# The last gate row's sums inside the attention, and plain heads that come out of the values product already turned

## The chip, the cores and the metric

The kernel is one program on 1 core of a Trainium2 chip. The metric is the device time of one launch in microseconds (us). The kernel before was timed three times: median 944.96 us, lowest 944.74, highest 946.05.

## What is computed

The reference is two layers of a diffusion backbone over 256 latent and 256 context tokens of width 1024, everything in float32. Layer 0 is a convolution and pooling mixer followed by a mixture of experts. Layer 1 is attention followed by a mixture of experts, and it gives out the latent tokens only. Every sublayer has a norm, a shift and scale from conditioning vectors (six rows per layer: shift, scale and gate of either sublayer), and a gate on its output. What matters here is cut from the reference:

```
def attend(q, k, v, scale):
    s = einsum(q, k) * scale
    p = softmax(s)
    return einsum(p, v)

o_m = attend(q_m, k_m, v_m, MLA_SCALE)                  # 4 plain heads
a1, a2 = attend(q1, k1, v_d, ..), attend(q2, k2, v_d, ..)
o_d = rms_norm(a1 - lam * a2, g_sub) * (1.0 - lam_init) # 4 differential heads
y = concatenate([o_m, o_d]) @ w_out
x = x + mod[1, 2] * y
x = x + mod[1, 5] * moe(modulate(rms_norm(x), mod[1, 3], mod[1, 4]))
```

The moe of a layer has 32 experts in 8 groups of 4; a token uses 2 experts of one group. All the weights of every expert are read once in a layer, whatever tokens it gets.

## The kernel before, in words

Each engine runs one program that is written out by hand, and semaphores order them. The names below are the kernel's.

**Weights.** SyncE (SP) issues all weight transfers in the order of `stream_plan` (133 units of up to 2 MB, numbered n below). `slot_plan` gives every unit a place: seven ring slots (0 to 6) and, for expert weights alone, four lent places: WORK_SLOT (7), X_SLOT (8), B_SLOT (9), PART_SLOT (10). SP goes through the units in order and, ahead of each, waits until the place is free (`load`, with `freed` for what the last unit of that place was read by); so a unit that has to wait holds all later ones. Units 81 and 82 are the two halves of `mod 1 5`, the weights of the moe gate row of layer 1. Units 83 and 84 are `wout`, the output projection of layer 1. From unit 85 on come the experts of layer 1: 85 `gu 0`, 86 `gu 1`, 87 `gu 2`, 88 `gu 3`, 89 `down 0`, 90 `gu 4`, 91 `gu 5`, 92 `down 1`, 93 `gu 6`, 94 `gu 7`, 95 `down 2`. With these eleven units all eleven places are full; unit 96 needs the place of unit 85, which is free when the first expert step is done. Before, 88 goes to WORK_SLOT and 89 to B_SLOT, and both wait for the last `o_turned` of the attention; 90 and 91 go to slots 6 and 3, which held units 81 and 82 and are free when these have been summed.

**Conditioning rows of layer 1.** Rows 2 to 5 are products of a vector of 1024 with a 1024 x 1024 matrix, made on VectorE: `mod_sum(n)` (L1882) multiplies a 128x512 piece of the weights with a per-partition scalar and adds it to a running sum (L1897; the first of a row is the plain product, L1895). Each row takes 16 such passes. The 48 passes of rows 2, 3 and 4 lie between the steps of the layer's projections. The 16 passes of row 5 (n = 48 to 63) stand in `add_out(1)`, ahead of the first two output tiles: ten ahead of tile 0 and six ahead of tile 1. TensorE adds up the partitions in `sum_moe_rows` (L1067, the product L1072) after the third tile of the output projection (`project_out`, L1150).

**Attention.** There are 16 units in `UNITS`: 0 to 7 plain (a head and a block of 128 queries each), 8 to 15 differential (two maps each). The engines run a software pipeline over an index i:

- TensorE (`attention_pe`), in iteration i: `probs(i-2)` turns the map, four 128x128 transposes (L570); `scores(i+1)`, for the plain units two at a time (L552, L555), for the differential ones four 64-row products (L561); `values(i-3)` (L581), whose stationary operand is the turned map and whose moving operand is the values, so that the result has queries in rows; `turn_o(i-5)` (L588) turns this result back.
- VectorE (`attention_vector`), in iteration i: `output_rows(i-3)` multiplies the result by one over the sum of the map's row (L1844; L1842 in the differential heads, with the norm's factor, too); `maxima(i+2)` (L1816, L1818); `normalize(i+1)` (L1825 takes the reciprocal of the sum; for a differential unit L1828 and L1830 form the difference of the two maps). The maps of the plain units are not divided before they are turned.
- ScalarE (`attention_scalar`), in iteration i: `exps(i)` (L664), `o_squares(i-3)` in the differential heads (L680), `o_cols(i-5)` copies the turned result to `oT` (L672), `turned_probs(i-1)` (L686).
- GpSimd takes the root for the differential heads and, before the attention, fetches the bias of row 5 into WORK (L2378).

`link` makes the next VectorE instruction wait for the one before it.

**After the attention** come the output projection in four tiles (L1150), the second norm, the router, then rows stored to memory and gathered by expert group, and the 16 expert steps, in each of which TensorE needs two `gu` units and one `down` unit.

## Time and profile before

| | |
|---|---|
| median of three runs | 944.96 us (944.74 to 946.05) |
| the profiled execution's own time | 942.52 us |
| its span | 940.9 us |
| mean granted TensorE clock | 0.956 of full speed |
| busy: TensorE, VectorE, ScalarE, GpSimd | 840.2, 362.6, 168.2, 178.1 us |
| moved by DMA | 297.99 MB, 317 GB/s on average |
| attention (first score product to last turned result) | 615.2 to 669.3 us of the span |
| output projection (L1150) | 669.4 to 700.0 us of the span |

The profile is of one execution. Its span leaves out 1.6 us that the execution's own time has. Times in the rows below are from the start of the span. A row of a timeline has the start, the duration, the engine, the line and the shapes; instructions of one group that follow each other are merged, with their number, and then the duration is that of the whole run. PE is TensorE, PEld its weight loads, DVE VectorE, ACT ScalarE, POOL GpSimd, SPq the queue of SyncE.

### The profile page before, as it was taken

The numbers are of one execution on the slowest core, as the hardware profiler recorded it, in microseconds if no ns is written. First come the engines' busy times: TensorE is split into PE (matmuls) and PEld (weight loads), VectorE is DVE, ScalarE is ACT, GpSimd is POOL, SyncE is SP. The second block draws the span as 40 slices with busy tenths as digits, with TensorE's granted clock in tenths as the row PEclk, the third lists the DMA queues.
The fourth block names the chain that finished last, engine by engine and source line by source line (L and its number), as shares of the span: only waits on it lengthen the run. The fifth ranks groups of instructions, "written<-read, shape, count | busy, mean of one in ns | idle before, by whom it ended". The sixth has DMA issues, their size and how long they took to land.

```text
span 940.9 us, 10044 instructions
## 1 busy us (share of the span) xinstructions
PE 840.2 (89%) x3735; PEld 372.3 (40%) x3735; DVE 362.6 (39%) x764; ACT 168.2 (18%) x415; POOL 178.1 (19%) x214
## 2 busy tenths in 40 slices
PE   4899999999999999878859999789899999778886
PEld 1444445447433333223238444446445333222222
DVE  1279998217111211110223686648624111111011
ACT  2301012216100000000032111538323000000000
POOL 2100292221220222211131321401211111011001
PEclk9999999999999999999959999989999999889888
DMA  8999354717999999999989469310577999999993
GB/s 363 409 416 399 142 213 194 286 72 277 339 402 400 365 405 395 401 397 418 420 329 424 163 231 370 134 71 1 212 302 257 408 400 406 416 418 424 414 417 162
DMA packets 34038, 297.99 MB, mean 317 GB/s; under 512 B 6624, under 2 KB 6930, under 8 KB 16316
## 3 DMA queue, kind: packets, MB, share of 16 engines
q1 hardware_dynamic: 26928, 283.26, 74.8%
q0 software_dynamic: 6976, 13.93, 4.2%
q8 instruction: 38, 0.62, 0.3%
q14 instruction: 20, 0.16, 0.0%
q10 hardware_dynamic: 76, 0.02, 0.0%
HBM read 293.67 MB, written 12.58 MB: 325 GB/s over the span
## 4 chain that ended last, share of the span: by engine, by line
PE 47%; DMA 24%; DVE 12%; issue 5%; SPq 5%; ACT 3%; PEld 2%; POOL 1%; PEldq 0%; DVEq 0%; POOLq 0%; ACTq 0%
PE bank L1275 11%; DVE WORK L2210 10%; DMA ring<-in_gu_pack 9%; PE bank L495 9%; PE bank L1300 6%; PE bank L1425 5%; DMA B<-in_gu_pack 5%; SPq L975 5%; DMA ring<-in_down_pack 4%; DMA ring<-in_win_pack 3%; PE bank L1150 3%; PE bank L1372 2%; PE bank L581 2%; DMA h_rows<-B 1%; PE bank L552 1%
## 5 line engine op out<-in xcount | busy, mean ns | idle before, releaser
L1275 PE MATMUL bank<-ring,hT 128*64 128x512 f32 x704 | 220.0, 633 | 25.1 <-DMA ring<-in_gu_pack 12.8
L2124 DVE SCALAR_TENSOR_TENSOR hT<-hT,WORK,bank 128x256 f32<-128x256 f32 x34 | 16.3, 481 | 326.3 <-ACT hT L1575 326.3
L1275 PEld LDWEIGHTS bank<-ring,hT 128*64 128x64 f32 x704 | 64.5, 145 | 125.2 <-issue 124.7
L2210 DVE SCALAR_TENSOR_TENSOR WORK<-WORK,par 128x512 f32<-128x512 f32 x116 | 90.7, 858 | 0.0
L495 PE MATMUL bank<-ring,hT 128*128 128x512 f32 (+2 forms) x256 | 88.0, 499 | 0.7 <-ACT hT L1538 0.7
L1300 PE MATMUL bank<-ring,WORK 128*64 128x512 f32 x336 | 76.3, 596 | 2.8 <-DMA ring<-in_down_pack 1.7
L1275 PE MATMUL bank<-WORK,hT 128*64 128x512 f32 x128 | 63.9, 645 | 5.0 <-issue 3.5
L1580 ACT ACTIVATE WORK<-bank 128x256 f32<-128x256 f32 x34 | 13.1, 384 | 282.9 <-PE bank L1284 282.9
L495 PEld LDWEIGHTS bank<-ring,hT 128*128 128x128 f32 x256 | 46.0, 190 | 35.8 <-issue 34.0
L1372 PE MATMUL bank<-hT,ring 128*128 128x512 f32 x128 | 57.7, 610 | 1.9 <-DMA ring<-in_win_pack 1.9
L1425 PE MATMUL bank<-ring,B 128*128 128x512 f32 x128 | 56.6, 596 | 0.8 <-DVE B L2227 0.8
L1275 PE MATMUL bank<-X,hT 128*64 128x512 f32 x104 | 49.5, 622 | 5.9 <-issue 3.1
L857 POOL DMA_INDIRECT hT<-h_rows,smalli x21 | 20.1, 959 | 174.2 <-PE bank L1249 80.5
L2255 POOL TENSOR_SCALAR small<-small 128x1 f32<-128x1 f32 (+2 forms) x46 | 13.5, 294 | 181.4 <-DVE small L1739 62.5
L1275 PE MATMUL bank<-B,hT 128*64 128x512 f32 x96 | 43.6, 597 | 1.0 <-issue 1.0
L1034 PE MATMUL bank<-ring,cs 128*32 128x512 f32 x256 | 33.9, 666 | 9.7 <-DMA ring<-in_mod_pack 8.5
L1300 PEld LDWEIGHTS bank<-ring,WORK 128*64 128x64 f32 x336 | 23.2, 137 | 45.1 <-issue 40.9
L1372 PEld LDWEIGHTS bank<-hT,ring 128*128 128x128 f32 x128 | 24.6, 195 | 33.4 <-issue 30.9
L870 POOL DMA_INDIRECT latents<-WORK,smalli x8 | 8.2, 1023 | 153.5 <-DVE WORK L2142 153.5
L2256 POOL TENSOR_TENSOR small<-small,cst 128x1 f32<-128x1 f32 (+2 forms) x46 | 35.8, 777 | 3.8
L1425 PEld LDWEIGHTS bank<-ring,B 128*128 128x128 f32 x128 | 23.8, 190 | 31.2 <-issue 27.7
L1575 ACT ACTIVATE hT<-bank 128x256 f32<-128x256 f32 x34 | 13.1, 384 | 124.9 <-PE bank L1275 121.0
(312 smaller groups left out, 1086.0 us busy)
## 6 DMA issues: line engine op xcount, KB each, us to landing
ring<-in_gu_pack SPq DMA_DIRECT2D x39, 2048.0 KB, 21.3
ring<-in_mod_pack SPq DMA_DIRECT2D x24, 2048.0 KB, 11.5
ring<-in_down_pack SPq DMA_DIRECT2D x19, 2048.0 KB, 25.5
WORK<-in_gu_pack SPq DMA_DIRECT2D x6, 2048.0 KB, 23.5
ring<-in_wout_pack SPq DMA_DIRECT2D x4, 2048.0 KB, 12.7
ring<-in_gu_pack SPq DMA_DIRECT2D x8, 1024.0 KB, 28.6
ring<-in_win_pack SPq DMA_DIRECT2D x3, 2048.0 KB, 37.0
X<-in_gu_pack SPq DMA_DIRECT2D x3, 2048.0 KB, 29.8
```

What stands on the lines that cost most here:

```text
L495: mm = pe.matmul(dst[:, 0:hi - lo], hT[:, k, t * P:(t + 1) * P], w[:, k, :], start=k == 0, stop=k == KC - 1)
L581: mm = pe.matmul(bank[VBANK[i % 2]][:, 0:P], PT[i % 2][:, c * P:(c + 1) * P], v[:, c, h * P:(h + 1) * P], start=c == 0, stop=c == 3)
L857: return pool.indirect_dma_start(XG[s], None, h2d[:, :], bass.IndirectOffsetOnAxis(ap=smalli[0:ST, i:i + 1], axis=0), bounds_check=rows_ - ...
L975: sp.dma_start(dst, src).then_inc(sem(f"weights_in{at}"), 16)
L1034: mm = pe.matmul(bank[b][at:at + 32, :], cs[:, k, :], w, start=k < 2, stop=k >= KC - 2)
L1150: mm = pe.matmul(bank[OUT_BANKS[L][i % 2]][:, :], lhs(k, j), w[:, k, :], start=k == 0, stop=k == KC - 1)
L1275: mm = pe.matmul(dst[ST * x:ST * x + ST, :], HG[L][s][:, k, :], columns(units[x], 512 * k, 512), start=k == 0, stop=k == KC - 1)
L1300: mm = pe.matmul(bank[5 + s][ST * h:ST * h + ST, :], HET[s][:, f, ST * x:ST * x + ST], columns(n, 2048 * x + 1024 * f + 512 * h, 512), sta ...
L1372: mm = pe.matmul(b[:, :], w[:, k, 256 * part + P * (m % 2):256 * part + P * (m % 2) + P], hT[:, k, :], start=k == 0, stop=k == KC - 1)
L1425: mm = pe.matmul(bank[OUT_BANKS[0][i % 3]][:, :], mixT[:, (k + 4) % KC, j * P:(j + 1) * P], w[:, (k + 4) % KC, :], start=k == 0, stop=k == ...
L2210: ins = dve.scalar_tensor_tensor(out=acc, in0=src, scalar=w, in1=acc, op0=ALU.mult, op1=ALU.add)
L2256: pool.tensor_tensor(dst, dst, C("half", 0, 1).to_broadcast([P, n]), ALU.pow).then_inc(sem(name), 1)
```

## The change

Three things are edited.

1. The 16 `mod_sum` passes of row 5 leave `add_out(1)` and stand in VectorE's attention loop, two behind `normalize(i+1)` in each of the iterations 0 to 7.
2. In the plain units the map is divided by its sum ahead of the turn: behind the reciprocal comes a `link` and a 128x512 multiplication in place on VectorE. `values` then takes the values as stationary operand and the turned map as moving operand, so that the result has queries in columns. `output_rows` and `turn_o` are left out for units 0 to 7, and ScalarE copies the result from its bank to `oT` at i-3 instead of i-5.
3. In `slot_plan` the places of `mod 1 5` no longer count as late. Units 88 and 89 then go to slots 6 and 3, and 90 and 91 to WORK_SLOT and B_SLOT; the same four places trade their later units in the same way. The wait of the lent places is for 8 `o_turned` instead of 16, since only the differential units are turned.

The diff:

```diff
--- before.py
+++ after.py
@@ -181,7 +181,7 @@
         if n > where_second and (not expert or WORK_SLOT not in free):
             free.sort(key=order)
         if expert and WORK_SLOT not in free:
-            late = [at for at in free if stream[held[at]][0] == "wout" or stream[held[at]][:3] == ("mod", 1, 5)]
+            late = [at for at in free if stream[held[at]][0] == "wout"]
             soon = [at for at in free if at not in late]
             if u[1] == 0:
                 free = soon + [WORK_SLOT] + late + [X_SLOT, B_SLOT, PART_SLOT]
@@ -351,6 +351,7 @@
         MOD_BANK = (6, 6, 6, 6, 6, 6, 7, 6)
         PBANK = (0, 1, 4, 5)
         VBANK = (5, 7)
+        PLAIN = 8
 
         UNITS = [(0, 2 * a + b, t) for a in range(2) for t in range(2) for b in range(2)] + [(1, h, t) for h in range(4) for t in range(2)]
 
@@ -573,17 +574,22 @@
             def values(i):
                 d, h, t = UNITS[i]
                 pe.wait_ge(sem("pt_done"), i + 1)
-                if i >= 2:
-
-                    pe.wait_ge(sem("o_rows"), i - 1)
-                v = VD if d else VM
+                if 2 <= i < PLAIN + 2:
+
+                    pe.wait_ge(sem("o_cols"), i - 1)
+                elif i >= 2:
+                    pe.wait_ge(sem("o_rows"), i - 1 - PLAIN)
                 for c in range(4):
-                    mm = pe.matmul(bank[VBANK[i % 2]][:, 0:P], PT[i % 2][:, c * P:(c + 1) * P], v[:, c, h * P:(h + 1) * P], start=c == 0, stop=c == 3)
+                    p, v = PT[i % 2][:, c * P:(c + 1) * P], (VD if d else VM)[:, c, h * P:(h + 1) * P]
+                    if d:
+                        mm = pe.matmul(bank[VBANK[i % 2]][:, 0:P], p, v, start=c == 0, stop=c == 3)
+                    else:
+                        mm = pe.matmul(bank[VBANK[i % 2]][:, 0:P], v, p, start=c == 0, stop=c == 3)
                 mm.then_inc(sem("pv_mm"), 1)
 
             def turn_o(i):
-                pe.wait_ge(sem("o_rows"), i + 1)
-                if i:
+                pe.wait_ge(sem("o_rows"), i + 1 - PLAIN)
+                if i > PLAIN:
                     pe.wait_ge(sem("o_cols"), i)
                 pe.transpose(bank[6][:, 0:P], OR[i % 2], ident).then_inc(sem("o_turned"), 1)
 
@@ -597,7 +603,7 @@
                     values(i - 3)
                 if i == n_units + 2:
                     sum_rows()
-                if 0 <= i - 5:
+                if PLAIN <= i - 5:
                     turn_o(i - 5)
 
         def attention_scalar(act, gate_rows):
@@ -667,15 +673,19 @@
 
             def o_cols(i):
                 d, h, t = UNITS[i]
-                act.wait_ge(sem("o_turned"), i + 1)
-                scale = subs[:, 0:1] if d else 1.0
-                act.activation(oT[:, 4 * d + h, t * P:(t + 1) * P], bank[6][:, 0:P], ACT.Identity, scale=scale).then_inc(sem("o_cols"), 1)
+                to = oT[:, 4 * d + h, t * P:(t + 1) * P]
+                if d:
+                    act.wait_ge(sem("o_turned"), i + 1 - PLAIN)
+                    act.activation(to, bank[6][:, 0:P], ACT.Identity, scale=subs[:, 0:1]).then_inc(sem("o_cols"), 1)
+                else:
+                    act.wait_ge(sem("pv_mm"), i + 1)
+                    act.activation(to, bank[VBANK[i % 2]][:, 0:P], ACT.Copy).then_inc(sem("o_cols"), 1)
 
             def o_squares(i):
                 j = i % 2
                 act.wait_ge(sem("pv_mm"), i + 1)
-                if i >= 2:
-                    act.wait_ge(sem("o_turned"), i - 1)
+                if i >= PLAIN + 2:
+                    act.wait_ge(sem("o_turned"), i - 1 - PLAIN)
                 u = 2 * (i % 8)
                 act.activation(OR[j], bank[VBANK[j]][:, 0:P], ACT.Square, scale=ri[:, u:u + 1], accum_out=oss[:, j:j + 1]).then_inc(sem("o_squares"), 1)
 
@@ -688,9 +698,11 @@
             for i in range(n_units + 5):
                 if i < n_units:
                     exps(i)
-                if 0 <= i - 3 < n_units and UNITS[i - 3][0]:
+                if PLAIN <= i - 3 < n_units:
                     o_squares(i - 3)
-                if 0 <= i - 5:
+                elif 0 <= i - 3 < PLAIN:
+                    o_cols(i - 3)
+                if PLAIN <= i - 5:
                     o_cols(i - 5)
                 if 0 <= i - 1 < n_units:
                     turned_probs(i - 1)
@@ -945,7 +957,7 @@
                 elif at == WORK_SLOT and STREAM[n][1] == 0:
                     sp.wait_ge(sem("mix_done"), 4)
                 elif at == WORK_SLOT or at == B_SLOT and STREAM[n][1] == 1:
-                    sp.wait_ge(sem("o_turned"), len(UNITS))
+                    sp.wait_ge(sem("o_turned"), len(UNITS) - PLAIN)
                 elif at == X_SLOT:
 
                     L = STREAM[n][1]
@@ -1829,28 +1841,30 @@
                                                   in1=es[:, o:o + 1], op0=ALU.mult, op1=ALU.mult))
                     ins = dve.scalar_tensor_tensor(out=EX[:, i % 2, 0, :], in0=EX[:, i % 2, 1, :], scalar=ri[:, u + 1:u + 2],
                                                    in1=EX[:, i % 2, 0, :], op0=ALU.mult, op1=ALU.add)
+                else:
+                    link(ins)
+                    ins = ts(EX[:, i % 2, 0, :], EX[:, i % 2, 0, :], ri[:, u:u + 1], None, ALU.mult)
                 ins.then_inc(sem("probs_ready"), 1)
 
             def output_rows(i):
                 dve.wait_ge(sem("pv_mm"), i + 1)
                 dve.wait_ge(sem("probs_ready"), i + 1)
                 scale = ri[:, 2 * (i % 8):2 * (i % 8) + 1]
-                if i >= 2:
-                    dve.wait_ge(sem("o_turned"), i - 1)
-                if UNITS[i][0]:
-                    dve.wait_ge(sem("o_rstd"), i - 7)
-                    ins = ts(OR[i % 2], bank[VBANK[i % 2]][:, 0:P], scale, ors[:, i % 2:i % 2 + 1], ALU.mult, ALU.mult)
-                else:
-                    ins = ts(OR[i % 2], bank[VBANK[i % 2]][:, 0:P], scale, None, ALU.mult)
-                ins.then_inc(sem("o_rows"), 1)
+                if i >= PLAIN + 2:
+                    dve.wait_ge(sem("o_turned"), i - 1 - PLAIN)
+                dve.wait_ge(sem("o_rstd"), i + 1 - PLAIN)
+                ts(OR[i % 2], bank[VBANK[i % 2]][:, 0:P], scale, ors[:, i % 2:i % 2 + 1], ALU.mult, ALU.mult).then_inc(sem("o_rows"), 1)
 
             for i in range(-2, n_units + 3):
-                if 0 <= i - 3:
+                if PLAIN <= i - 3:
                     output_rows(i - 3)
                 if i + 2 < n_units:
                     maxima(i + 2)
                 if 0 <= i + 1 < n_units:
                     normalize(i + 1)
+                if 0 <= i < KC:
+                    mod_sum(6 * KC + 2 * i)
+                    mod_sum(6 * KC + 2 * i + 1)
 
         @block.vector
         def _(dve):
@@ -1976,9 +1990,6 @@
                         last = i == 2 * nj - 1
                         if i >= 2:
                             dve.wait_ge(sem("x_added"), 8 * L + i - 1 + last)
-                        if L == 1 and i < 2:
-                            for n in (range(6 * KC, 6 * KC + 10), range(6 * KC + 10, 8 * KC))[i]:
-                                mod_sum(n)
                         dve.wait_ge(sem("out_mm"), 8 * L + i + 1)
                         tt(OUTT[L][i % 2], bank[OUT_BANKS[L][i % len(OUT_BANKS[L])]][:, :], GB[:, streams[j // 2], 512 * h:512 * h + 512], ALU.mult).then_inc(sem("out_used"), 1)
                         if last:
```

## Rows read from the trace of the kernel before

**Rows 1.** The page: the span

```profile
span 940.9 us, 10044 instructions
```

**Rows 2.** Chain that ended last, in time: start, us, what

```profile
649.94 1.06 PE bank L561 x4
651.00 1.09 PE bank L581 x8
652.20 0.44 PE bank L570 x4
...
669.38 22.56 PE bank L1150 x48
...
792.94 48.55 DMA ring<-in_gu_pack
```

**Rows 3.** Windows: busy of PE, PEld, DVE, ACT, POOL; clock, DMA share, GB/s

```profile
608.00:611.00 3.00, 1.37 (x6) 0.50 (x4) 2.52 (x10) 1.37 (x5) 1.28 (x3) 1.00 0.42 98
...
622.94:643.05 20.11, 19.33 (x113) 12.31 (x114) 11.20 (x34) 11.69 (x30) 0.00 (x0) 1.00 0.00 1
643.05:657.11 14.06, 14.06 (x92) 9.43 (x92) 13.53 (x36) 12.24 (x39) 2.25 (x6) 1.00 0.00 0
...
670.00:673.00 3.00, 3.00 (x5) 1.24 (x4) 2.67 (x5) 0.30 (x1) 0.00 (x0) 0.50 0.91 322
...
695.00:700.00 5.00, 5.00 (x14) 2.19 (x13) 0.00 (x0) 1.75 (x4) 0.74 (x2) 1.00 0.26 108
```

**Rows 4.** Timeline: VectorE's multiplications of 128x512, in the projections and in `add_out(1)`

```profile
566.98 0.88 DVE L1895 TENSOR_SCALAR B<-ring,cs 128x512 f32<-128x512 f32 x2
...
670.34 6.71 DVE L1897 SCALAR_TENSOR_TENSOR WORK<-ring,cs,WORK 128x512 f32<-128x512 f32 x10 [1.14 <-ACT GB L1557]
678.25 0.69 DVE L1983 TENSOR_TENSOR hT<-bank,GB 128x512 f32<-128x512 f32 x1 [1.20 <-PE bank L1150]
678.85 5.07 DVE L1897 SCALAR_TENSOR_TENSOR WORK<-ring,cs,WORK 128x512 f32<-128x512 f32 x6
```

**Rows 5.** Timeline of VectorE, a plain iteration (622.94) and an output row (628.82)

```profile
622.94 0.69 DVE L1816 TENSOR_REDUCE small<-bank 128x1 f32<-128x512 f32 x1 [1.08 <-PE bank L555]
623.74 0.15 DVE L1825 RECIPROCAL small<-small 128x1 f32<-128x1 f32 x1
623.81 0.67 DVE L1816 TENSOR_REDUCE small<-bank 128x1 f32<-128x512 f32 x1
...
628.82 0.35 DVE L1844 TENSOR_SCALAR WORK<-bank,small 128x128 f32<-128x128 f32 x1
629.09 0.68 DVE L1816 TENSOR_REDUCE small<-bank 128x1 f32<-128x512 f32 x1
```

**Rows 6.** Timeline of VectorE, one differential iteration, and the pass of L1842

```profile
643.05 1.27 DVE L1816 TENSOR_REDUCE small<-bank 128x1 f32<-128x512 f32 x2
644.44 0.16 DVE L1825 RECIPROCAL small<-small 128x2 f32<-128x2 f32 x1
644.63 0.22 DVE L1828 SCALAR_TENSOR_TENSOR small<-small 128x1 f32<-128x1 f32 x1
645.55 0.35 DVE L1844 TENSOR_SCALAR WORK<-bank,small 128x128 f32<-128x128 f32 x1
...
651.13 0.41 DVE L1842 TENSOR_SCALAR WORK<-bank,small 128x128 f32<-128x128 f32 x1
651.46 1.28 DVE L1816 TENSOR_REDUCE small<-bank 128x1 f32<-128x512 f32 x2
```

**Rows 7.** Timeline of SP's queue: start, time in the queue, units

```profile
668.95 0.33 SPq L975 DMA_DIRECT2D WORK<-in_gu_pack  x1
...
700.05 0.33 SPq L975 DMA_DIRECT2D ring<-in_gu_pack  x1
...
724.13 0.33 SPq L975 DMA_DIRECT2D B<-in_down_pack  x1
```

**Rows 8.** DMA issues, 560 to 800 us: size and median us to landing

```profile
WORK<-in_mod_b POOLq DMA_DIRECT2D x1, 4.0 KB, 2.1
```

## The prediction, made before the changed kernel was run

> **What bounds the kernel now.** I read the page first, for the span [rows 1], then the chain of waits in order of time, to see which stage is bound by what [rows 2]. Three stages matter. In the attention the chain stays on TensorE from product to product. In the output projection it is TensorE again: 48 products in 22.56 us. From 793 us it is a wait of 48.55 us for weights: the last fifth is bound by transfers. The windows [rows 3] then tell how full each engine is. From 622.94 to 643.05 TensorE is busy 19.33 of 20.11 us, and VectorE 11.20. From 643.05 to 657.11, the differential units, VectorE has 13.53 of 14.06: TensorE is full, and VectorE has hardly anything left either. That is what decides here, since the change puts work on VectorE at just this place.
>
> **Why the old place of the 16 passes costs nothing.** In the output projection ten passes take 6.71 us, and then VectorE waits 1.20 us for the first tile; six more follow in 5.07 us [rows 4]. TensorE needs about 7 us for a tile (22.56 us for three, with a slow start) and doesn't wait for them. Taking them out of there gains 0.
>
> **VectorE's new loop, iteration by iteration.** I take distances between starts, since durations overlap. A plain iteration of before: from the maximum (622.94) to the reciprocal (623.74) 0.80 us, then 0.07 to the next maximum (623.81) [rows 5]. New in it:
> - *The division.* It waits for the reciprocal. From a reciprocal to an instruction that waits for it are 0.19 us (644.44 to 644.63) [rows 6] instead of 0.07. The trace has no such division in place, but it has two products of 128x512 with a per-partition scalar, from SBUF to SBUF: 0.88 us for two, each 0.48 long, thus 0.40 from start to start [rows 4]. I take 0.40. Bounds: 0.27, the pitch of a 128x128 pass (628.82 to 629.09) [rows 5], and 0.66, that of the passes with two tensors (below).
> - *Two passes.* Ten take 6.71 us, the last of them 0.75 (their own duration; it moves the pitch by 0.01): 0.66 or 0.67 a pass, 1.33 for two. The six behind them have (5.07 - 0.75) / 5 = 0.86 a pass, while GpSimd adds tiles next to them [rows 4]. GpSimd is idle (0.00) in the new place from 622.94 to 643.05 [rows 3], so 0.66 holds there; 0.86 is the upper bound.
>
> So a plain iteration becomes 0.80 + 0.19 + 0.40 + 1.33 = 2.72 us, and there are six of them (iterations 0 to 5). Iteration 6 has the two maxima of a differential unit, 1.39 us to the reciprocal [rows 6], and divides the last plain map: 1.39 + 0.19 + 0.40 + 1.33 = 3.31. Iteration 7 is wholly differential; before, it takes 2.50 (643.05 to 645.55) without an output row [rows 6], with two passes 3.83. Sum: 6 x 2.72 + 3.31 + 3.83 = 23.46 us. Before, the same eight iterations take 643.05 - 622.94 = 20.11. VectorE comes to the maximum of unit 10 **3.35 us late**: 12.93 us of work are added (10.64 of passes, seven divisions at 0.52, less five output rows at 0.27), and of the 20.11 only 9.58 were idle (six times 0.87, 1.46, 2.50 and the five output rows are the rest).
>
> Do other engines hide or lengthen this? TensorE loses eight turns at 0.11 us (652.20 - 651.00 - 1.09 [rows 2]), 0.9 us in all; its unit is then 1.06 + 1.09 + 0.44 = 2.59 us, under VectorE's 2.72, so VectorE sets the pace from about iteration 3, and the 0.9 us are hidden. At first TensorE is ahead by its position in the pipeline and would wait only from the eighth map on, some 1.1 us for each of two maps. ScalarE (11.69 of 20.11 us) has room, and loses copies from one place to another only. The new orientation of the values product has the same four products of 128x128: 0.
>
> **What is caught up.** Output rows 5, 6 and 7 are gone from iterations 8, 9 and 10: these take 2.50, 2.50 and, with the first differential output row in front of the next maximum (0.33, 651.13 to 651.46), 2.83 us, 7.83 in all, where before it was 651.46 - 643.05 = 8.41 [rows 6]. 0.58 us come back. From the maximum of unit 13 on both kernels do the same on an engine that has nothing to spare, and the tail behind the last map is a chain that the change leaves alone. **The attention ends 3.35 - 0.58 = 2.8 us later**, at about 672.
>
> **Are the earlier weights worth something?** Units 88 and 89 wait until 668.95 now [rows 7], and would go out at about 634 and 646, when 8 and 16 passes are done, into queues that carry nothing (share 0.00) [rows 3]. But what they fill are places, not time. Units 85 to 95 fill all eleven places; 93 goes at 700.05, when the output projection is through, 95 at 724.13 [rows 7], and the share falls to 0.26 between 695 and 700 [rows 3]: what could be fetched had been fetched, before 93 could go. 96 waits for the first expert step in both kernels. Gain 0. From 724 on the same bytes follow at the same rate, so that stage shifts as a whole with its start, and nothing absorbs the 2.8 us: they stand in front of everything that frees a place. Waiting for 8 turns instead of 16 is the same event.
>
> **Sum.** Passes +10.64, divisions +3.64, the first five output rows -1.35, idle time filled -9.58, caught up later -0.58: +2.8 us. The profiled execution took 942.52 us with a span of 940.9, so 945.3; the median of the runs is 944.96, 2.4 us above it, and the forecast for the median is 944.96 + 2.8 = **947.8 us**, +0.3%. A measurement of this kernel can tell about 0.2%, 1.9 us.
>
> **Against a rule, the division.** The row gives 0.40 us of pitch and 0.48 of duration. The Trainium skill, page "VectorE: DVE Perf Modes", section on the TRN2 errata, gives 58 cycles and half a cycle for each of 512 elements in such a product, which is an estimate of 0.33 us; with that as the pitch, seven divisions would cost 0.5 us less in all and the sum would be +2.3. The trace stands above it, and the page itself says that its constant is too low.
>
> **Rivals.**
> 1. *VectorE has the slack, or TensorE stays the bound: no difference.* If the division costs 0.27 and the waits between engines overlap better than a chain of starts shows, 0.9 us come off; if in addition the lateness at unit 10 is caught up by TensorE's lead, no more than the 0.9 us of turns is left, as a gain. That gives -0.9 to +1.9 us, 944.1 to 946.8. For it: 2.72 us of VectorE against 2.59 of TensorE in a plain unit is near the edge. Against: VectorE's 13.53 of 14.06 us later on leave no room to catch up.
> 2. *Faster, by the earlier weights.* Mechanism: two transfers of 2 MB less lie in front of unit 93 and the stores of rows behind the output projection; if one of these, or of the gathers, is late now because queues still carry old weights, it comes earlier, and with it unit 96. It decides if the queues are still behind at 700 us. Price: one transfer, 2 MB at the run's mean of 317 GB/s, 6.6 us, which is set against the 2.8: 947.8 - 6.6 = 941.2. Against it is the 0.26 before 700 us [rows 3].
> 3. *Slower still: TensorE's clock.* From 670 to 673 us, behind the attention's tail, the granted clock is 0.50 of full, the 1.2 GHz level [rows 3]. In the changed loop it waits for VectorE twice, 1.1 us in some 3 each. If the clock goes to the lower level for a stretch of 3 us there, 2.59 us of products take up to 5.2 and one or two units come 1.5 to 3 us later, past VectorE's pace: 949.3 to 950.8. With passes at the bound of 0.86 the same end is met: 16 x 0.20 = 3.2 us more, 951. The Trainium skill, page "TensorE: Matmul & The Clock Gate", section "A second HAM failure mode: psum-queue depth-cycling", says that small idle gaps between groups of products can make the clock go back and forth; by that rule this rival would hold. The trace speaks rather against: from 608 to 611 us TensorE is busy 1.37 of 3 us, less than it would be here, and the clock is 1.00 [rows 3].
> 4. *The change doesn't do what it says:* the first pass in the loop waits for the bias row and holds VectorE. It lands 2.1 us after its issue [rows 8], which follows the last turn of the projections, and the first pass comes only after the first two maps have been scored: nothing for it. It would give back the old time, 945.0, at the best.
>
> **How the numbers follow.** Forecast 0.58 (946.6 to 949.0), rival 1 0.22, rival 2 0.08, rival 3 0.11, rival 4 0.01. 944.1 to 950.8 takes in the forecast, rival 1 and most of rival 3, and leaves out rival 2. Slower by over 0.2% is above 946.85: most of the forecast and all of rival 3, 0.66. Within 0.2% is 943.07 to 946.85: rival 1 and the forecast's lower edge, 0.25. Faster: 0.09.
>
> **What would show it.** Right: VectorE without gaps from the maximum of unit 2 to that of unit 10, plain maxima 2.7 us apart, that of unit 10 at 646.4; division 0.48 long; passes 0.66 apart; TensorE waiting for the divided map (L570) in iterations 7 to 10; SP sends 88 and 89 at about 634 and 646, and 93, 95 and 96 each 2.8 us later than before; the output projection as long as before (30.6 us). Wrong: gaps left on VectorE in these eight iterations, an output projection that is shorter, less than 2.8 us between the end of the attention and unit 95 against before, or a granted clock under 1.00 between 640 and 660.

## The result, and the profile after

The changed kernel takes 947.12 us in the median of 12 runs, the kernel before 944.85 in 12 runs, 2.3 us less. The ratio on record, which isn't the quotient of these two medians, is 1.0030, 95% interval 1.0016 to 1.0043, which is 2.8 us slower (1.5 to 4.1). The forecast for the median was 947.8, of slower by 2.8. Single runs of either kernel spread over 5 to 7 us, so the ratio counts here and not one run against another. Below, a difference over the run is always the recorded ratio times the median of the kernel before in the same measurement.

The page of the profiled execution (948.5 us, 1.4 above its median), to be set beside [rows 1]:

```profile
span 946.8 us, 10008 instructions
```

The span is 5.9 us longer than in [rows 1], more than twice the effect. The stages show why. VectorE's timeline in the attention loop of the changed kernel, the first iteration with passes, one of the plain ones, then iterations 6 and 7 (L1828 is L1816 of before, L1837 is L1825, L1846 the new division, L1911 the passes):

```profile
628.05 0.69 DVE L1828 TENSOR_REDUCE small<-bank 128x1 f32<-128x512 f32 x1 [0.57 <-PE bank L556]
...
633.47 0.68 DVE L1828 TENSOR_REDUCE small<-bank 128x1 f32<-128x512 f32 x1
634.19 0.15 DVE L1830 TENSOR_SCALAR small<-small 128x1 f32<-128x1 f32 x1
634.26 0.15 DVE L1837 RECIPROCAL small<-small 128x1 f32<-128x1 f32 x1
634.45 0.49 DVE L1846 TENSOR_SCALAR GB<-GB,small 128x512 f32<-128x512 f32 x1
634.85 1.41 DVE L1911 SCALAR_TENSOR_TENSOR WORK<-ring,cs,WORK 128x512 f32<-128x512 f32 x2
636.18 0.68 DVE L1828 TENSOR_REDUCE small<-bank 128x1 f32<-128x512 f32 x1
...
644.29 1.28 DVE L1828 TENSOR_REDUCE small<-bank 128x1 f32<-128x512 f32 x2
647.60 1.28 DVE L1828 TENSOR_REDUCE small<-bank 128x1 f32<-128x512 f32 x2
651.44 1.28 DVE L1828 TENSOR_REDUCE small<-bank 128x1 f32<-128x512 f32 x2
```

A plain iteration takes 636.18 - 633.47 = 2.71 us (forecast 2.72), iteration 6 takes 3.31 (3.31), iteration 7 takes 3.84 (3.83). The division is 0.49 long with the next start 0.40 behind it (0.40). From the maximum of unit 2 to that of unit 10 are 651.44 - 628.05 = 23.39 us (23.46) instead of 20.11 [rows 5, 6], and behind 628.05 no row of VectorE in this stretch has a wait. TensorE's timeline, on the other hand, has waits now where the maps of units 8 and 9 are to be turned (L571):

```profile
650.25 0.66 PE L571 MATMUL bank<-cst,GB 128*128 128x128 f32 x4 [0.72 <-DVE GB L1842]
654.09 0.66 PE L571 MATMUL bank<-cst,GB 128*128 128x128 f32 x4 [1.03 <-DVE GB L1842]
```

Windows of the changed kernel (columns as in [rows 3]): the eight iterations, the stretch in which TensorE waits, the start of the output projection, and the time before unit 93 can go:

```profile
622.94:646.40 23.46, 22.49 (x114) 12.38 (x112) 20.10 (x48) 11.78 (x30) 0.00 (x0) 0.99 0.23 89
650.00:655.00 5.00, 3.72 (x22) 2.41 (x24) 4.90 (x11) 3.17 (x10) 0.00 (x0) 1.00 0.52 157
677.70:680.70 3.00, 3.00 (x4) 1.27 (x5) 0.00 (x0) 0.88 (x2) 0.00 (x0) 0.57 0.82 262
700.00:705.00 5.00, 5.00 (x14) 2.02 (x14) 0.69 (x1) 3.17 (x5) 2.00 (x3) 1.00 0.02 7
```

The clock stays at 1.00 while TensorE waits (3.72 of 5 us busy). The transfers do run inside the attention now (a share of 0.23 instead of 0.00), and before unit 93 goes (708.33) the queues are nearly empty: 0.02 here, 0.01 in the last 5 us ahead of it, where [rows 3] has 0.26. In the chain and on SP's queue (compare [rows 2, 7]):

```profile
677.66 22.56 PE bank L1162 x48
...
799.90 48.24 DMA ring<-in_gu_pack
```

```profile
651.55 0.33 SPq L987 DMA_DIRECT2D ring<-in_down_pack  x1
677.23 0.33 SPq L987 DMA_DIRECT2D WORK<-in_gu_pack  x1
...
708.33 0.33 SPq L987 DMA_DIRECT2D ring<-in_gu_pack  x1
...
731.43 0.33 SPq L987 DMA_DIRECT2D B<-in_down_pack  x1
```

Unit 89 goes at 651.55, 17 us before even unit 88 went in [rows 7], and unit 95 at 731.43, 7.3 us later. Of these 7.3, 5.4 lie ahead of the attention already: its first score product starts at 620.57 instead of 615.15. What the change did must be read inside the stages. The table is worked out from the timelines of all profiles; the columns are distances in us: from the start of VectorE's scaling (L1818 of before, L1830 here) of unit 2's maximum to that of unit 10 (a), from there to unit 15 (b), from there to the first product of the output projection (c, the tail), the output projection up to the first turned tile (d), and the sum a + b + c against the kernel before. The labels are those of the experiments below. Some 8 us of the attention lie ahead of unit 2 and are in no column; they vary from execution to execution (8.5 and 8.3 in two profiles of the kernel before, 8.2 and 8.9 in two of the changed one, 9.8 in e3).

```
kernel                       a      b      c      d   a+b+c    ratio to before
before                   20.69  14.07  10.95  30.47      0
before, second profile   20.69  14.08  10.96  30.47    0.0   1.0003 (0.9987 to 1.0019)
changed                  23.97  13.53  11.38  30.47   +3.2   1.0030 (1.0016 to 1.0043)
changed, second          23.97  13.53  11.38  28.77   +3.2   1.0028 (1.0012 to 1.0044)
passes alone (e1, e9)    23.07  14.03  10.96  28.78   +2.4   1.0003, 1.0006
division alone (e2)      20.50  13.75  11.02  28.78   -0.4   0.9994 (0.9978 to 1.0011)
places of before (e3)    23.97  13.54  11.38  28.77   +3.2   1.0031 (1.0017 to 1.0045)
third pass (e4)          29.27  13.52  11.04  28.78   +8.1   1.0084 (1.0062 to 1.0107)
one pass (e7)            21.22  13.50  11.03  30.47    0.0   1.0005 (0.9991 to 1.0019)
division + tail (e8)     20.49  13.76   9.77  28.78   -1.7   0.9965 (0.9953 to 0.9977)
before + tail (e10)      20.70  14.07   9.82  28.77   -1.1   0.9972 (0.9956 to 0.9988)
changed + tail (e11)     23.97  13.52   9.94  28.77   +1.7   0.9995 (0.9979 to 1.0010)
before, busy tail (e12)  20.69  14.06  11.91  28.78   +1.0   0.9994 (0.9979 to 1.0008)
```

Columns a, b and c repeat to 0.02 us between two profiles of one kernel, while the interval of the run's time is 0.12 to 0.17% wide to either side with 12 runs.

### The profile page after: what moved, and what is told of

It is laid out like the page before. It is cut to its first block, busy times and chain, and to the rows that moved or that the text cites. A ratio compares the mean times of both kernels' runs of the same rounds, so it can differ in the third digit from the quotient of the medians.

```text
span 946.8 us, 10008 instructions
## 1 busy us (share of the span) xinstructions
PE 842.1 (89%) x3727; PEld 374.3 (40%) x3727; DVE 362.5 (38%) x764; ACT 168.9 (18%) x415; POOL 177.9 (19%) x214
## 4 chain that ended last, share of the span: by engine, by line
PE 50%; DMA 20%; DVE 16%; issue 6%; ACT 3%; SPq 2%; PEld 2%; POOL 1%; another core or an unknown queue 0%; PEldq 0%; DVEq 0%; POOLq 0%; ACTq 0%
PE bank L1287 15%; DVE WORK L2221 10%; PE bank L496 9%; DMA ring<-in_gu_pack 9%; PE bank L1312 7%; PE bank L1437 5%; DMA B<-in_gu_pack 5%; DMA ring<-in_win_pack 3%; PE bank L1162 3%; PE bank L1384 2%; SPq L987 2%; DVE small L1828 1%; DVE WORK L1911 1%; DMA h_rows<-B 1%; PEld bank L1287 1%
## 5 line engine op out<-in xcount | busy, mean ns | idle before, releaser
L1287 PE MATMUL bank<-ring,hT 128*64 128x512 f32 x688 | 208.9, 627 | 25.5 <-DMA ring<-in_gu_pack 17.7
L1287 PEld LDWEIGHTS bank<-ring,hT 128*64 128x64 f32 x688 | 61.6, 144 | 118.7 <-issue 118.4
L1312 PE MATMUL bank<-ring,WORK 128*64 128x512 f32 x368 | 83.5, 596 | 1.6 <-ACT WORK L1592 1.6
L1287 PE MATMUL bank<-WORK,hT 128*64 128x512 f32 x128 | 61.5, 625 | 7.8 <-issue 6.3
L1287 PE MATMUL bank<-X,hT 128*64 128x512 f32 x112 | 53.8, 627 | 3.6 <-DMA B<-in_gu_pack 2.8
L1312 PEld LDWEIGHTS bank<-ring,WORK 128*64 128x64 f32 x368 | 25.6, 137 | 48.4 <-issue 45.0
```

Source lines behind the costliest of these rows:

```text
L1287: mm = pe.matmul(dst[ST * x:ST * x + ST, :], HG[L][s][:, k, :], columns(units[x], 512 * k, 512), start=k == 0, stop=k == KC - 1)
L1312: mm = pe.matmul(bank[5 + s][ST * h:ST * h + ST, :], HET[s][:, f, ST * x:ST * x + ST], columns(n, 2048 * x + 1024 * f + 512 * h, 512), sta ...
```

## The experiments

**The two parts, the places, and a third pass.** The first, e1, is the kernel before with the passes in the loop:

```diff
                 if 0 <= i + 1 < n_units:
                     normalize(i + 1)
+                if 0 <= i < KC:
+                    mod_sum(6 * KC + 2 * i)
+                    mod_sum(6 * KC + 2 * i + 1)
...
-                        if L == 1 and i < 2:
-                            for n in (range(6 * KC, 6 * KC + 10), range(6 * KC + 10, 8 * KC))[i]:
-                                mod_sum(n)
```

> The kernel before with the 16 passes of the gate row in the attention loop, two in each of the iterations 0 to 7, and nothing else: plain heads and places as before. My theory (VectorE's chain of starts): a plain iteration has 0.87 + 1.33 + 0.27 = 2.47 us, less than TensorE's 2.7 to 2.85, so iterations 0 to 5 hide it; iteration 6 has 1.46 + 0.27 + 1.33 = 3.06 and iteration 7 has 2.50 + 0.27 + 1.33 = 4.10, from unit 8's maximum to unit 10's 7.16 where it was 5.47: the attention ends 1.7 us later and the run is 1.7 us slower (about 946.6). Rival (VectorE had the slack): attention and run as before, under 0.5 us. Rival (the old place did cost something, or the transfers gain): faster than before.

Measured: the attention is 2.35 us longer behind unit 2, where 1.7 was expected, and the ratio is 1.0003 (0.9989 to 1.0016). VectorE's timeline shows where the expectation was 0.7 short:

```profile
629.71 0.69 DVE L1816 TENSOR_REDUCE small<-bank 128x1 f32<-128x512 f32 x1 [0.34 <-PE bank L555]
...
635.42 0.69 DVE L1816 TENSOR_REDUCE small<-bank 128x1 f32<-128x512 f32 x1 [0.76 <-PE bank L555]
...
640.29 1.28 DVE L1816 TENSOR_REDUCE small<-bank 128x1 f32<-128x512 f32 x2
```

TensorE makes the scores of plain units two at a time, so VectorE can't use the 0.34 and 0.76 us in front of a pair. From unit 6's maximum it has two iterations of 2.43 us in a row, and comes to unit 8 at 640.29, 15.35 us behind unit 2's maximum, where the kernel before takes 14.64. It is 0.7 late before the two expensive iterations begin. An average of 2.47 against 2.85 us a unit had hidden that. The edit e2 is the changed kernel with the passes and the places put back:

```diff
-                if 0 <= i < KC:
-                    mod_sum(6 * KC + 2 * i)
-                    mod_sum(6 * KC + 2 * i + 1)
...
+                        if L == 1 and i < 2:
+                            for n in (range(6 * KC, 6 * KC + 10), range(6 * KC + 10, 8 * KC))[i]:
+                                mod_sum(n)
...
-            late = [at for at in free if stream[held[at]][0] == "wout"]
+            late = [at for at in free if stream[held[at]][0] == "wout" or stream[held[at]][:3] == ("mod", 1, 5)]
```

> The changed kernel with the 16 passes back in front of the first two output tiles and the places as before: the plain heads with the division ahead of the turn and without the turn back, alone. My theory: a plain iteration has 0.87 + 0.52 = 1.39 us on VectorE against 2.59 on TensorE, so the divisions are hidden; TensorE saves up to eight turns at 0.11 us, and iterations 8 to 10 lose an output row each on VectorE (2.50 instead of 2.77); the attention ends 0.7 to 0.9 us earlier, and the run is 0.8 us faster (about 944.1). Rival (the longer way from the reciprocal to the turned map delays TensorE in each unit): no gain or up to 1 us slower.

Measured: 0.44 us less in the attention, half of what was expected, and no difference in the run that the interval could tell. In e2's chain the plain and differential units follow each other on TensorE at its own pace, without waits (two units of it):

```profile
641.39 1.06 PE bank L562 x4
642.45 1.09 PE bank L587 x8
643.54 0.44 PE bank L571 x4
643.98 1.06 PE bank L562 x4
645.04 1.09 PE bank L587 x8
646.12 0.44 PE bank L571 x4
```

The pace is 2.59 us, as forecast. Some of the saved turns are lost again at the start, where unit 1's map is turned 1.63 us behind unit 0's instead of 1.44, since it waits for its division; the rest of what is missing was not followed up. So the division by itself is hidden. Beside the passes it isn't: with the passes alone a + b + c grows by 2.4 us, with both by 3.2, for the division costs VectorE 0.52 us a unit, and the output row that falls away in its place gives back only 0.27. The places (e3) are the changed kernel with the second of these lines put back, and nothing else:

```diff
-            late = [at for at in free if stream[held[at]][0] == "wout"]
+            late = [at for at in free if stream[held[at]][0] == "wout" or stream[held[at]][:3] == ("mod", 1, 5)]
```

> The changed kernel with the places of the units as before (units 88 and 89 in the lent places, 90 and 91 in slots 6 and 3): four transfers go out behind the attention again. My theory (what is fetched early fills places and gains no time): attention as in the changed kernel (57.1 us from the first score product to the first output product), run within 0.5 us of the changed kernel. Rival (the earlier weights took transfers out of the way and gave something back): slower than the changed kernel by 1 us or more, with a longer stretch between the end of the output projection and the issue of unit 95 (23.1 us in the changed kernel, 24.1 in the kernel before).

Measured: columns a to d as in the changed kernel, and 1.0031 beside 1.0030 and 1.0028. The stretch from the output projection to unit 95 is 24.6 us, against 23.2 and 23.3 in the changed kernel, but 23.6 and 24.3 in two profiles of the kernel before. Over all profiles it is 23.2 to 24.2 in the four with the new places (e4 and e11 among them) and 23.5 to 24.7 in the others. The profiles leave open whether the new places are worth some tenths of a us, and the run's time shows nothing. Earlier weights gain nothing that can be measured. The third pass (e4):

```diff
+                if 0 <= i < KC:
+                    dve.scalar_tensor_tensor(out=wk[:, 1024:1536], in0=wk[:, 1536:2048], scalar=cs[:, i, 1:2], in1=wk[:, 1024:1536], op0=ALU.mult, op1=ALU.add)
```

> The changed kernel with a third pass of 128x512 in each of the iterations 0 to 7, over a part of WORK that nothing else uses then; its result is not used. My theory (VectorE sets the pace of these eight iterations from the first on): each costs its full 0.66 us, the stretch from unit 2's maximum to unit 10's grows from 23.4 to 28.7 us, the attention and the run by 5.3 us against the changed kernel (about 952.6). Rival (TensorE or ScalarE sets part of the pace): less than 4 us. Rival (TensorE's clock falls while it waits): granted clock under 1.00 inside the attention and more than 6 us.

Measured: column a grows from 23.97 to 29.27, by 5.30 us for eight passes, 0.66 each; the median of 6 runs is 951.2, 7.2 above before and 5.3 above e3, which has two passes and was measured with it. By the ratio it is 7.9 us slower than before (5.9 to 10.1), where a + b + c says 8.1. VectorE sets the pace of these iterations alone, and the delay comes out at the end of the run in full, within that interval. The clock stays at 1.00 here as well. Of the windows of 3 us from 622 us on, this is the one in which TensorE is least busy:

```profile
652.00:655.00 3.00, 1.31 (x9) 0.79 (x9) 2.89 (x7) 1.97 (x6) 0.00 (x0) 1.00 0.80 300
```

**Repetition, and one pass.** Both kernels were run again, e5 and e6.

> The kernel before itself, to see what of a stage's length is the kernel's and what the execution's. All theories: ratio 1.000 within the interval. From unit 2's to unit 10's maximum 20.7 us as in the first profile. If the lower clock behind the attention (output projection 30.5 us instead of 28.8 in the runs with one part alone) belongs to the execution and not to the kernel, it can be absent here.

> The changed kernel itself, once more, beside its parts on the same chip. My theory: 0.3% slower than before (+2.3 to +2.8 us); from unit 2's to unit 10's maximum 24.0 us again, from unit 10's to unit 15's 13.5. Rival (the 5 us that the first profile shows ahead of the attention belong to the change): the first score product again at 620 us instead of 615 to 617.

Measured: all columns as before but for d. In e6 the first score product starts at 617.9 (before again: 616.3, the other kernels 614.7 to 617.4), so most of the 5 us ahead of the attention belonged to that execution. With one pass an iteration (e7; the other eight stand in front of the first output tile):

```diff
-                if 0 <= i < KC:
-                    mod_sum(6 * KC + 2 * i)
-                    mod_sum(6 * KC + 2 * i + 1)
+                if 0 <= i < KC:
+                    mod_sum(6 * KC + i)
```

> The changed kernel with one pass instead of two in each of the iterations 0 to 7, the other eight in front of the first output tile, places as before. My theory (a threshold: what fits under TensorE's 2.59 us a unit is free, what goes beyond it costs in full): a plain iteration has 0.87 + 0.52 + 0.66 = 2.05 us and is hidden; iterations 6 and 7 have 2.64 and 3.16, 5.80 together, where TensorE needs 5.18 for two units: from unit 2's to unit 10's maximum 21.1 us, against 20.5 without a pass and 24.0 with two; run 0.3 us above before at most (944 to 944.5). Rival (every pass costs the same): half of what two cost, 22.2 us in that stretch and 1.5 us slower than before.

Measured: 21.22 us in column a, 21.1 expected. With no pass, one, two and three, column a is 20.50, 21.22, 23.97 and 29.27: the first costs 0.7 for eight, the second 2.8, the third its full 5.3. This is a threshold, not a price per instruction. In a + b + c the kernel with one pass is level with the kernel before (0.0), since the turns and output rows saved pay for it.

**The tail.** The profiles point to something outside the change: behind the last map stands a chain of TensorE, ScalarE, GpSimd and VectorE, and in its middle TensorE adds up the partitions of another gate row. That is 1.72 us in front of the turn that unit 15's squares wait for. It was moved behind that turn, in the kernel with the division alone (e8), in the kernel before (e10) and in the changed one (e11):

```diff
-                if i == n_units + 2:
-                    sum_rows()
                 if PLAIN <= i - 5:
                     turn_o(i - 5)
+                if i == n_units + 2:
+                    sum_rows()
```

> The kernel with the division alone (passes and places as before), and the four products that add up a gate row's partitions behind the attention's last differential units moved by one place: behind the turn of unit 13 instead of ahead of it. The last unit's squares on ScalarE wait for that turn. My theory (the tail is a chain TensorE - ScalarE - GpSimd - VectorE - TensorE with 1.7 us of foreign products in it): from unit 15's maximum to the first output product 9.8 us instead of 11.0, run 1.2 us below the division alone and 1.5 to 2 us below before (about 942.3). Rival (the products then delay the turn of units 14 and 15 as much): no difference to the division alone.

> The kernel before with the gate row's four products behind the turn of unit 13 and nothing else. My theory: from unit 15's maximum to the first output product 9.7 us instead of 10.95, the run 1.2 us faster or somewhat more, and the division adds 0.4 us to it in e8. Rival (the 3.3 us of e8 need both edits together): under 0.5 us.

> The changed kernel with the gate row's four products behind the turn of unit 13. My theory: the change's cost stands by itself: against the kernel with the same tail and without the passes in the loop (e8) 3.0 to 3.5 us more from unit 2's maximum to the first output product, the run 1.2 us or somewhat more below the changed kernel, about as before (943.5 to 945). Rival (the tail hides part of the passes' lateness): as fast as e8.

TensorE's timeline of e8, where the turn of unit 13 (L594, 664.66) now stands ahead of the products (L1077):

```profile
663.59 1.13 PE L585 MATMUL bank<-X,WORK 128*128 128x128 f32 x8
664.66 0.30 PE L594 MATMUL bank<-cst,WORK 128*128 128x128 f32 x1
664.80 1.94 PE L1077 MATMUL bank<-MR,cst 128*128 128x512 f32 x4
666.58 0.27 PE L594 MATMUL bank<-cst,WORK 128*128 128x128 f32 x1
667.40 0.30 PE L594 MATMUL bank<-cst,WORK 128*128 128x128 f32 x1 [0.55 <-ACT B L679]
```

Measured: the tail is 9.8 instead of 11.0 us in e8 and e10. The run is 0.35% faster in e8 (interval 0.23 to 0.47) and 0.28% in e10 (0.12 to 0.44), both faster than either kernel of this study. That is 3.3 us (2.2 to 4.4) and 2.6 us (1.1 to 4.2), while a + b + c is only 1.7 and 1.1 us shorter. Both profiles have the shorter column d as well, 1.7 us less; the next part comes to it. The changed kernel with the same tail (e11) lies at 0.9995 and 3.4 us above e8 in a + b + c: the cost of the passes stands by itself.

**What e1 loses in the attention and not over the run.** It was measured again (e9).

> The kernel before with the 16 passes in the attention loop and nothing else, once more: its attention was 2.35 us longer from unit 2's maximum to the first output product, but its median lay only 0.3 us above before (interval 1.0 below to 1.5 above). My theory (nothing behind the attention absorbs a delay, and the first measurement drew low): the same 2.35 us inside the attention, and 1 to 3 us over the run. Rival (here something behind the attention gives 2 us back that the changed kernel does not give back): again under 1 us over the run.

Measured: the same 2.35 us inside, and 1.0006 (0.9992 to 1.0019), about 0.6 us, 1.8 at the most. e1 had 0.3, 1.5 at the most. The rival holds against the kernel before: something gives back about 2 us. Column d has a candidate. In both profiles of the kernel before, in the first one of the changed kernel and in e7 the output projection takes 30.47 us, in the ten other kernels' and repetitions' profiles 28.8. The windows at its start, first of the kernel before, then of e1:

```profile
669.40:672.40 3.00, 3.00 (x4) 1.27 (x5) 2.06 (x4) 0.90 (x2) 0.00 (x0) 0.58 0.83 262
```

```profile
673.70:676.70 3.00, 2.98 (x7) 1.44 (x8) 0.00 (x0) 0.94 (x2) 0.00 (x0) 1.00 0.78 246
```

A granted clock of 0.58 against 1.00, four products recorded against seven, and 1.7 us. If column d is added to a + b + c, the sum comes within 0.5 us of the run's time for e1, e8, e9, e10, e11 and e12, but lies 1.2 to 1.6 us under it for e2, e3, e4 and e6: one profile doesn't tell how often the other 11 runs had the low clock. The last run put products into TensorE's idle time in the tail (e12):

```diff
+                for _ in range({n_units + 2: 8, n_units + 3: 6}.get(i, 0)):
+                    pe.matmul(bank[4][:, 0:P], ident, ident, start=True, stop=True)
```

> The kernel before with 14 products of 128x128 whose result nobody reads, 8 behind the turn of unit 13 and 6 behind that of unit 14, where TensorE waits 0.96 and 0.81 us. Both profiles of the kernel before have the granted clock at 0.56 to 0.58 in the first 3 us of the output projection (30.5 us long), eight of the ten other kernels' profiles have it at 1.00 there (28.8 us); e1 and e9 have 2.35 us more in the attention and lost only 0.3 and 0.7 us over the run. My theory (that low clock follows TensorE's idle time in the tail and costs the kernel before 1.7 us in most of its executions, which some of the edited kernels escape): the output projection is 28.8 us long here, the tail at most 0.3 us longer, and the run 1 to 1.7 us faster. Rival (whether the clock falls belongs to the execution and not to what TensorE does in the tail): the low clock stays in the profile, or the run's time is as before.

(Of the other kernels' profiles at that time it was nine of eleven that had the clock at 1.00, not eight of ten.) TensorE's timeline and the window at the start of the output projection:

```profile
666.20 1.95 PE L603 MATMUL bank<-cst 128*128 128x128 f32 x16
667.99 0.27 PE L588 MATMUL bank<-cst,WORK 128*128 128x128 f32 x1
668.10 1.50 PE L603 MATMUL bank<-cst 128*128 128x128 f32 x12
```

```profile
671.00:674.00 3.00, 3.00 (x8) 1.33 (x7) 2.88 (x5) 0.09 (x1) 0.00 (x0) 1.00 0.75 306
```

Measured: the clock stays at 1.00 and d is 28.78, but each product counts twice in the timeline (28 for 14), so the filling is longer than the gaps and the tail grows by 0.95 us. The run is at 0.9994 (0.9979 to 1.0008), 0.6 us faster, where the sum of both would be 0.7; the interval (2.0 faster to 0.8 slower) holds both that and no effect. The expected 1 to 1.7 us with a tail at most 0.3 longer did not come. Nor does the clock of this one profile show that the filling kept it up, since nine of eleven profiles without it had 1.00 too. All four profiles with TensorE busy 2.0 us or more of the 3 ahead of the projection (e8, e10, e11, e12) have 1.00, and four of the ten with 0.8 have not; that fits the theory and is too few to show it.

## Why the prediction was right, step by step

- *VectorE's loop*: 23.46 us forecast, 23.39 measured, each of its terms within 0.01 us. A price from another place (0.40 for the division, 0.66 for a pass) held where the shape and the memories were the same and GpSimd was idle (0.00 in the window). The estimate of 0.33 us for the division from the Trainium skill (page "VectorE: DVE Perf Modes", section on the TRN2 errata) was too low; the page itself says that its formula comes out low.
- *What hides what*: TensorE waits for the differential maps of units 8 and 9, 0.72 and 1.03 us, where 1.1 each was forecast. The prediction had them begin at the eighth map (unit 7, the last divided one); that one is turned at 646.42 without a wait. The saved turns bring nothing in the changed kernel, and 0.4 us where the passes are away (e2).
- *What is caught up*: column b is 0.54 us shorter, 0.58 was forecast.
- *The tail* was taken to be left alone, and is 0.43 us longer. In both profiles of the changed kernel the values product of unit 15 waits 0.34 us for VectorE's output row of unit 13 (L1856), a wait that the kernel before does not have there. From the first:

```profile
670.25 0.55 POOL L2267 TENSOR_TENSOR small<-small,cst 128x1 f32<-128x1 f32 x1
671.29 0.41 DVE L1856 TENSOR_SCALAR WORK<-bank,small 128x128 f32<-128x128 f32 x1 [1.17 <-POOL small L2267]
671.85 1.13 PE L585 MATMUL bank<-X,WORK 128*128 128x128 f32 x8 [0.34 <-DVE WORK L1856]
```

The row starts 0.49 us behind the end of GpSimd's factor; in the kernel before it is 0.13 us, and 0.13 to 0.14 in e4 and e7, which have the division and passes in the loop too and tails of 11.0 us. What holds VectorE back in the changed kernel is open. From unit 2 on the attention takes 3.2 us longer, not 2.8.
- *Over the run* 2.8 us (1.5 to 4.1) and in the repetition 2.6 (1.1 to 4.2) were lost. The forecast's 2.8 lies in both. That it is met so closely is in part luck: the attention lost 0.4 us more than forecast, and the intervals are over 2 us wide. One sign of being wrong did show: from the first product of the output projection to unit 95 the changed kernel takes 53.8 us and the kernel before 54.8, so that 1.0 of the delay was made up there, between units 93 and 95 (0.4 in the second pair of profiles). It may be the scatter seen with e3. "Nothing absorbs it" agrees with e4 within its interval. For e1 about 2 us came back. The low clock behind the attention is a candidate for that, seen in the profiles and not settled, since one profile a kernel can't say how often it comes. If the kernel before has it more often than the changed one (two of two profiles against one of two), the changed kernel's 3.2 us in the attention and 2.6 to 2.8 over the run agree, too.
- *The rivals*: slack on VectorE (1) falls with column a. Earlier weights (2) fall with e3. The lower clock (3) did not come where it was feared: 1.00 throughout the waits from 645 us on, though TensorE is busy only 3.72 of 5 us, and 1.00 in e4 with 1.31 of 3. The rule of the Trainium skill on short gaps (page "TensorE: Matmul & The Clock Gate", section "A second HAM failure mode: psum-queue depth-cycling") is not borne out in this stretch. The prediction's own argument against this rival was weaker than it looked, though. It took the window 608 to 611 of the kernel before, busy 1.37 of 3 us at a clock of 1.00, and left out the two behind it:

```profile
611.00:614.00 3.00, 1.30 (x6) 0.96 (x6) 2.67 (x13) 0.64 (x2) 0.02 (x1) 0.64 0.93 380
614.00:617.00 3.00, 2.27 (x4) 0.85 (x4) 0.00 (x0) 0.64 (x2) 1.56 (x2) 0.50 0.56 229
```

There the clock does fall, in 6 us (608 to 614) of which TensorE is busy 2.67, and the first score product starts at 615.15 in a window at 0.50. That the loop stayed at 1.00 was known only from the profile of the changed kernel. The bias row (4) was never waited for: the first pass follows its division by 0.40 us.

## What to carry to other kernels

Work that an engine does in another engine's shadow is free only as long as the shadow is longer than it. Before moving it, add up both engines' starts, iteration by iteration, in the new place as in the old: here the old place hid 16 passes fully (column d is 28.77 or 28.78 in ten profiles, with all 16 passes beside the projection in e2, e8, e10 and e12 and with none in the other six), and the new one had room for about eight (e7). Averages flatter such a sum where one engine delivers in pairs (e1). A buffer that is filled earlier is worth something only if the next unit in order could also go earlier; here all places were full, the next one waited for a computation, and no gain was measured (e3). And the tail of a pipeline deserves a look of its own: one instruction group behind the next turn gave 0.3%, about as much as the change cost.

## What the hardware showed beyond expectation

- From unit 2 on, the stretches of one kernel's attention repeat to 0.02 us between two profiled executions, while the run's time scatters by 1.2 to 2.1 us (standard deviation of 12 runs), and the start of the attention lay anywhere between 614.7 and 620.6 us of the span.
- The clock of TensorE behind the attention's tail differs between two profiles of one and the same kernel: 0.57 of full speed in the first 3 us of the output projection in the first profile of the changed kernel, 1.00 in the second, worth 1.7 us, with the same tail ahead of it to 0.01 us. In the four profiles that have it TensorE had been busy about 0.8 of the 3 us ahead of the projection, as in six of the ten that don't (2.0 or more in the other four), and the clock was still 1.00 in those 3 us.
